# Expert mixture of a streaming encoder layer: arguments of a column pair directly behind its second dot product, multiplies two columns behind the dot products, eight row buffers

## What is computed

```python
q = (t @ wq).reshape(blk, PEER_HEADS, PEER_DKEY)          # 8 heads
s1 = einsum('thd,hnd->thn', q[..., :half], subkeys[:, 0]); s2 = ...
v1, i1 = top_k(s1, 16); v2, i2 = top_k(s2, 16)
sc, pos = top_k(v1[..., :, None] + v2[..., None, :], 16)  # 16 of 256
e = i1[pos // 16] * 128 + i2[pos % 16]                    # expert numbers
g = softmax(sc)
a = gelu(einsum('td,thkd->thk', t, u[e]))
out = einsum('thk,thkd->td', g * a, v[e])
```

## Time and profile before

| | |
|---|---|
| median of 3 runs | 1940.57 us |
| lowest, highest | 1929.52, 1940.98 us |
| profiled execution | 1941.12 us, its span 1939.3 us |
| busy in the span | TensorE 67%, VectorE 68%, ScalarE 30%, GpSimd 27% |
| bytes moved | 704.63 MB, of them 570.46 MB by the gathers |
| mean granted TensorE clock | 0.751 |

### The profile page before, as it was taken

The page is one execution under the profiler, slowest core; times in us unless marked ns, Lnnn a source line. Parts: engine busy times, 40 slices in busy tenths (PEclk is TensorE's granted clock), DMA queues, the critical chain, the costliest instruction groups (busy, mean ns, idle before and its releaser), DMA issues.

```text
span 1939.3 us, 25847 instructions
## 1 busy us (share of the span) xinstructions
PE 1307.0 (67%) x8684; PEld 719.1 (37%) x8684; DVE 1325.8 (68%) x3948; ACT 576.1 (30%) x2040; POOL 523.8 (27%) x552
## 2 busy tenths in 40 slices
PE   8779884656887756578986765768877634444343
PEld 3457752234544422244553522445543311111111
DVE  3634228488986656779876775899866687686754
ACT  2223212242432222333432322433422222222222
POOL 0000003133333232333232322322332333343332
PEclk9878986967778878678779869678888855555555
DMA  5032348999999999999999999999999999999997
GB/s 203 6 134 88 120 141 352 401 378 424 424 425 424 403 420 414 378 403 425 366 424 422 424 423 398 393 425 359 369 424 423 425 426 426 427 426 422 426 423 317
DMA packets 122949, 704.63 MB, mean 363 GB/s; under 512 B 18368, under 2 KB 21488, under 8 KB 52672
## 3 DMA queue, kind: packets, MB, share of 16 engines
q0 software_dynamic: 78336, 570.46, 70.9%
q1 hardware_dynamic: 39968, 128.97, 17.4%
q10 hardware_dynamic: 4512, 3.54, 0.6%
HBM read 699.83 MB, written 3.02 MB: 362 GB/s over the span
## 4 chain that ended last, share of the span: by engine, by line
DMA 32%; PE 22%; DVE 21%; issue 15%; ACT 3%; POOL 1%; ACTq 0%; another core or an unknown queue 0%; DVEq 0%; POOLq 0%
DMA rows<-in_peer_uv,index 22%; DVE rows L2042 9%; PE ps_v L1397 6%; DMA wch<-in_w_tok 5%; PE ps_f L1241 2%; PE ps_h L1377 2%; DMA wch<-in_w_out 2%; PE ps_f L1291 2%; PE ps_f L1270 2%; PE ps_f L1104 2%; PE ps_f L1216 1%; POOL rows L1082 1%; DMA wch<-in_peer_wq 1%; PE ps_f L1256 1%; DVE score L1818 1%
## 5 line engine op out<-in xcount | busy, mean ns | idle before, releaser
L1082 POOL DMA_INDIRECT rows<-in_peer_uv,index x544 | 522.0, 960 | 1299.5 <-PE ps_v L1397 1022.0
L2042 DVE CUSTOM_DVE_ANT_0 rows<-rows,ps_h 128x1024 f32<-128x1024 f32 x544 | 657.3, 1220 | 275.9 <-DMA rows<-in_peer_uv,index 205.7
L1397 PE MATMUL ps_v<-rows,diag 128*32 128x256 f32 x4352 | 435.3, 514 | 444.1 <-ACT diag L1650 430.1
L1397 PEld LDWEIGHTS ps_v<-rows,diag 128*32 128x32 f32 x4352 | 127.9, 133 | 697.9 <-ACT diag L1650 566.5
L1641 ACT ACTIVATE tan<-arg 128x2 f32<-128x2 f32 x272 | 55.4, 204 | 858.3 <-DVE arg L2052 829.4
L1644 ACT ACTIVATE weight<-tan,lead 128x1 f32<-128x1 f32 x544 | 180.8, 379 | 9.1
L1650 ACT ACTIVATE diag<-sel,weight 128x32 f32<-128x32 f32 x544 | 140.7, 305 | 0.0
L1241 PEld LDWEIGHTS ps_f<-bufh,wch 128*128 128x128 f32 x768 | 115.5, 236 | 22.5 <-issue 20.2
L1241 PE MATMUL ps_f<-bufh,wch 128*128 128x128 f32 x768 | 122.1, 325 | 0.0
L1104 PE MATMUL ps_f<-wch,bufh 128*128 128x410 f32 x192 | 81.4, 556 | 42.1 <-DMA wch<-in_w_tok 39.2
L1104 PEld LDWEIGHTS ps_f<-wch,bufh 128*128 128x128 f32 x192 | 35.7, 203 | 84.1 <-DMA wch<-in_w_tok 41.7
(11 more groups left out here) (319 smaller groups left out, 1751.5 us busy)
## 6 DMA issues: line engine op xcount, KB each, us to landing
wch<-in_w_gate SPq DMA_DIRECT2D x64, 512.0 KB
wch<-in_w_tok SPq DMA_DIRECT2D x48, 410.0 KB
wch<-in_w_o SPq DMA_DIRECT2D x32, 512.0 KB
wch<-in_w_out SPq DMA_DIRECT2D x32, 512.0 KB
wch<-in_peer_wq SPq DMA_DIRECT2D x32, 512.0 KB
rows<-in_peer_uv,index POOLq DMA_INDIRECT x544
w_tok<-in_w_tok SPq DMA_DIRECT2D x4, 1640.0 KB, 13.4
wch<-in_keyb SPq DMA_DIRECT2D x6, 512.0 KB
```

Source lines behind the costliest of these rows:

```text
L1082: pool.indirect_dma_start(rows[c % RING][:, :, :].rearrange("p a d -> p (a d)"), None, io.peer_uv[:, :], at).then_inc(s_uv[c % RING], 16)
L1397: ins = nc.tensor.matmul(ps_v[GROUP * a:GROUP * (a + 1), :], diag[:, c % DRING, :], rows[c % RING][:, 1, QD * a:QD * (a + 1)], start=False ...
L2042: v.tensor_tensor_reduce(out=u, in0=u, in1=ps_h[:, :], scale=1.0, scalar=0.0, op0=ALU.mult, op1=ALU.add, accum_out=dots[:, c % KEEP:c % KE ...
```

## The change

Three things change together. On VectorE `arguments` of the pair b-1, b follows `dot(b)` directly at odd b, where it came behind the first dot product of the next pair. On ScalarE `diagonals` moves from even to odd iterations with it, and on TensorE and in `block_out` `LAG` is 2 in place of 3, so that every multiply stands one iteration earlier against the ticks. The ring has eight buffers in place of nine. No computing instruction is added or removed.

```diff
-RING = 9
+RING = 8
 DRING = 4
 KEEP = 32
-LAG = 3
+LAG = 2
@@ ScalarE
-                if 2 <= b <= NCOL and b % 2 == 0:
-                    diagonals(b - 2)
+                if b < NCOL and b % 2 == 1:
+                    diagonals(b - 1)
@@ VectorE
-            for b in range(NCOL + 1):
+            for b in range(NCOL):
...
-                if b < NCOL:
-                    dot(b)
-                if b >= 2 and b % 2 == 0:
-                    arguments(b - 2)
-                if b < NCOL:
-                    n, k = b // SG, b % SG
-                    for _ in range(ticks_at(b)):
-                        next(ahead)
-                    if n + 1 < NB and k % 2 == 0 and 1 <= k // 2 <= PARTS:
-                        choose(n + 1, k // 2 - 1)
+                dot(b)
+                if b % 2 == 1:
+                    arguments(b - 1)
+                n, k = b // SG, b % SG
+                for _ in range(ticks_at(b)):
+                    next(ahead)
+                if n + 1 < NB and k % 2 == 0 and 1 <= k // 2 <= PARTS:
+                    choose(n + 1, k // 2 - 1)
```

## The result

| | before | changed |
|---|---|---|
| median, first 9 runs of each | 1939.81 us | 1951.06 us |
| lowest to highest | 1929.52 to 1942.35 | 1939.12 to 1955.9 |
| ratio to before, 95% interval | | 1.0053 [1.0033, 1.0073] |
| second sample of the changed kernel, 6 runs | | 1947.05 us, 1.0058 [1.0042, 1.0074] |
| profiled execution, its span | 1941.12, 1939.3 | 1943.76, 1942.0 |

The changed kernel is slower by 0.55%, some 11 us. That lies inside the predicted range and within 1%, but it is clear of no change, and I had forecast no change. The two ratios are the measure; the profiled execution of the changed kernel was its second fastest of nine, so it shows less of the loss than a usual run does. Runs of these two kernels lie 13 and 17 us apart here, and a single trace can't be read for a difference of 11 us. What it can be read for is each step.

What follows compares the result with a forecast made beforehand. The prediction took the DMA engines as the bound, with the ring only a queue before them. Its terms 0 + 1 - 1 + 0 summed to 0, giving 1940.5 us, with an 8-in-10 range of 1927 to 1954.

Steps and rivals of the forecast that it cites:

- What bounds the kernel: Whole gather stretch: DMA engines are the bound, the full ring is not; better buffer handling can win 17 us at most.
- Part 1: Ring of eight, multiplies two behind: each buffer is freed at the same place of TensorE's queue; cost 0.
- Part 2: Arguments directly behind their dot on VectorE: a 0.12 us wait at 271 pairs, mostly hidden; 1 us, at most 9.
- Part 3: Choose parts and block boundaries: mean of gathers not yet used stays, some boundary waiting may go; -1 us.
- Part 4: Start and end: ninth gather goes out at some 316.0 us, the end is unchanged; cost 0.
- B: Choose parts with front work: less cover delays buffer release; slower, 1963 to 1972 us, half of it 1956; chance 0.12.
- A: DMA dips fill up through steadier VectorE work and earlier release at boundaries; 1924 us, half of it 1932; chance 0.11.
- C: Whole gather stretch: the ring is the bound, so eight buffers do eight ninths of the work; 2108 us; chance 0.03.

Runs made afterwards that it cites:

- before_wait_next: The kernel before, with a pair's arguments also waiting for the dot product just ahead of them on VectorE; ratio 1.0011 to the kernel before.
- changed_ring7: The changed kernel with seven row buffers in place of eight, multiplies still two behind; ratio 1.0078 to the kernel before.
- before_cube_four: The kernel before with the cube of each pair computed four times in a row, each waiting for the last; ratio 1.0204 to the kernel before.
- before_choose_odd: The kernel before with only the choose parts moved from even to odd iterations; ratio 1.0036 to the kernel before.

## Why the prediction was wrong, step by step

**What bounds the kernel: right, with one wrong conclusion.** Where there is no front work the DMA engines are the bound, and seven buffers don't change that. That no handling of buffers could win more than 17 us is not contradicted: the best kernel won 0.28 and 0.43%, 5 and 8 us. What was wrong is the step from a full queue in the last columns to "a ring that is always full is no bound": in the 384 columns with front work one buffer less costs 0.57% under the old order and 0.1 to 0.7% in six pairs of the new one, not all of them clear of noise, and 1.1% in a seventh, from eight to seven with lag 3.

**Part 1, "Cost: 0 ... the two counts agree exactly": this step failed.** With the changed order on VectorE and ScalarE, ring and lag together take the kernel from 1.0012 to 1.0053 and 1.0058, 0.4%, or 8 us. With the choose parts in odd iterations the same step costs as much, from 0.9998 (nine buffers, lag 3) to 1.0035 (eight, lag 2). Counting release and use in columns sets a column of lag equal to a buffer. The runs give for a column of lag, from 3 to 2: +0.15% at nine buffers (not clear of noise) and +0.3% at eight (slower), -0.5% at seven; with choose odd -0.33% at nine and none at eight. So a column of lag is no fixed price, and it isn't worth a buffer. My reading is that two things pull against each other: the column of cover that it gives, and TensorE standing closer behind the arguments, so that its front ticks wait behind VectorE's. The second is seen in the waits above, and in the old order, one column closer, the kernel lost 2.7%. How the two add up to the five numbers isn't shown. That cover is worth the more the less there is of it would fit the even choose phase with lag 3 (a buffer is worth 0.1%, then 1.1%), but not the odd one with lag 2 (0.7%, then 0.4%).

**Part 2, the wait: mechanism right, size probably too small.** 0.12 us was right at every pair. I took 1 us, with 9 as bound, since I let it act only in windows with idle DMA time. Measured directly it is 0.11%, 2 us, with an interval of -2 to 6, which doesn't refute the 1 us. Scaled down from the fourfold cube it is 0.12 x 192 x 0.29 = 7 us, or 8 us with 0.36. Both are estimates of the same term. I would now say 2 to 8 us, two or more times what I took. The Trainium skill (VectorE: DVE Perf Modes, The DRAIN you can't avoid) says that the semaphore costs nothing extra, from a measurement on a chain of copies; it does not hold for this pair of instructions, which the wait alone moves apart by 0.12 us. VectorE's busy time rose by 22 us with it, and not because more is computed: the cube no longer overlaps the 0.08 us of the accumulator read, and 272 x 0.08 = 22 us.

**Part 3, "The mean stays": this step failed too.** The mean of gathers in hand stays, but they are not needed evenly. What matters is the place of a choose part against the arguments: right behind them was better than one dot product ahead of the next ones. (That it stands between the two dots of a pair isn't the fault; in the old order it stands there too, and is better there.) Moving it to the worse place costs the old order 0.36%, and moving it back gives the changed kernel 0.2% and, with nine buffers, 0.7 and 0.5% (1.0028 and 1.0026 against 0.9957 and 0.9972). It gives nothing clear of noise with seven buffers or with lag 3 in the new order. The gain of 1 us at the boundaries didn't come; TensorE waits there more often.

**Part 4** was right: the ninth gather to 0.2 us, the end unchanged.

**The rivals.** B (less cover in the choose parts) was nearest, in mechanism and sign; it had 0.12 and was priced at 1956 for a half. A had no part in the changed kernel. C was refuted by seven buffers.

**What is settled and what isn't.** Along one path, the changed kernel is the kernel before plus: the wait (0.1%), the shift of the whole pattern by a column with a buffer less (from 1.0011 to 1.0035, 0.2%), and the choose phase (from 1.0035 to 1.0055, 0.2%). Along another: the new arguments (0.1%), a buffer (0.1%), the lag (0.3%). Each such step has a 95% interval of some 0.25% to either side, and the edits don't add up independently, so no single one is shown to carry the loss. Shown is that ring and lag together cost 0.4% in the new order, with either choose phase, that the choose phase costs in the old order by itself, that one buffer costs in the old order, and that next to nothing of the loss lies in the last 160 columns. By which mechanism ring and lag cost their 0.4% stays open. So does how much of the 0.2% in the middle of the first path is the block boundary wait; no kernel took that wait alone away, and the fastest one has 12 such waits itself.

**A version that beats both:** the new argument place, lag 2, nine buffers, choose in odd iterations: 1933.63 and 1932.78 us, 0.9957 and 0.9972 of before. Columns 0 to 384 take 1220.4 and 1217.7 us in its two traces, against 1226.5 before; the last 160 take 394.2.

## What to carry to other kernels

When a ring shrinks together with the distance between producer and consumer, the positions may match exactly and the time still not: ask also who now stands directly behind whom, and what long piece of work stands ahead of the release. Try the longest piece of a loop right behind the step that lets the buffers go, in place of ahead of it: here that was worth 0.2 to 0.7% with the multiply one iteration behind the arguments and eight or nine buffers, and nothing clear of noise otherwise. A queue that is seen to be full in one stage says nothing of its slack in another; a kernel with one buffer less is the cheap test for it, and it should be run before a buffer is given away.

## What the runs showed of the hardware

- A small VectorE instruction that waits for the one just ahead of it starts 0.11 or 0.12 us behind the accumulator read, in place of at the same instant; with it VectorE's busy time in the profile grows by 22 us over 272 pairs (1325.8 us in before, 1348.2 in before_wait_next), since the two no longer overlap.
- The indirect gathers of 1.05 MB hold the same rate with nine, eight and seven buffers, as long as nothing else is in the way (1600 to 1650 us: 426 GB/s in before, 426 in the changed kernel, 427 in changed_ring7; the windows after it down to 421 in these three): the 159 columns behind column 384 take 392.9 to 396.0 us, 2.47 to 2.49 us each, in all traces but that of before_cube_four (400.4).
- Executions of one kernel differ by 6 to 21 us of 1940 within a sample (4 to 12 runs; before_choose_odd has the 21). The mean granted clock doesn't tell them apart: the changed kernel's 1952.01 us had a mean of 0.760, its 1943.76 us one of 0.761.
